# Output projection of a hybrid encoder step: eight turns of a row tile's normalised rows move in between the last matmuls of the next tile

## The reference, cut to what matters

```python
mix = merge_branches(o_fox, o_swa, ga, gb, w_proj_fox[l], w_proj_swa[l], w_o[l])   # ends in ... @ w_o
xp = xp + rmsnorm(mix, norm_mix_post[l])
f, conv_state = conv_ffn(rmsnorm(xp, norm_ffn_pre[l]), zero_past, w_up[l], conv_w[l], conv_b[l], w_down[l])
```

## Time and profile before

| | us |
|---|---|
| median of 3 runs | 1555.41 |
| lowest, highest | 1554.9, 1557.6 |
| span of the profiled execution | 1553.1 |

### The profile page before, as it was taken

One profiled execution on the slowest core, in us unless ns is written; L12 is line 12 of the kernel. 1 busy time (PEld: TensorE's weight loads), 2 busy tenths in 40 slices (PEclk: granted clock), 3 DMA queues, 4 the chain that ended last, 5 costly groups with the idle time before them and its releaser, 6 DMA issues.

```text
span 1553.1 us, 25753 instructions
## 1 busy us (share of the span) xinstructions
PE 1495.8 (96%) x9803; PEld 1397.5 (90%) x9803; DVE 1020.4 (66%) x2016; ACT 607.5 (39%) x1256; POOL 611.0 (39%) x407
## 2 busy tenths in 40 slices
PE   6999999999999999999999999999999999999997
PEld 5889999999997998899788999999999999778885
DVE  6866667767674357867445896555555555578986
ACT  5143534435342235666223333333333332444463
POOL 6522232222222322225231568888888781000104
PEclk9999999999999999999999999999999999999999
DMA  6232222222132721129431122222222228723568
GB/s 199 63 94 74 74 87 65 73 70 70 30 97 75 233 95 38 56 82 291 156 108 58 45 67 86 83 83 83 70 83 68 71 83 278 240 97 116 170 195 156
DMA packets 156475, 165.41 MB, mean 107 GB/s; under 512 B 14005, under 2 KB 121913, under 8 KB 156353
## 3 DMA queue, kind: packets, MB, share of 16 engines
q1 hardware_dynamic: 119689, 109.34, 22.6%
q10 hardware_dynamic: 34840, 51.14, 10.0%
q0 software_dynamic: 1824, 3.28, 1.5%
HBM read 125.56 MB, written 39.85 MB: 107 GB/s over the span
## 4 chain that ended last, share of the span: by engine, by line
PE 80%; DVE 9%; DMA 3%; POOL 3%; ACT 2%; issue 2%; ACTq 1%; SPq 0%; DVEq 0%; POOLq 0%
PE bank L1138 16%; PE bank L1140 16%; PE bank L1139 16%; PE bank L1144 6%; PE bank L1146 6%; PE bank L1145 6%; PE bank L1170 4%; PE bank L1279 2%; PE bank L1250 1%; PE bank L1249 1%; DVE p L2649 1%; DVE rowsn L2408 1%; DVE p L2625 1%; POOL ring_l L1080 1%; PE bank L1629 1%
## 5 line engine op out<-in xcount | busy, mean ns | idle before, releaser
L1138 PE MATMUL bank<-ht_h,ring_h 128*128 128x352 f32 x816 | 268.9, 330 | 1.8 <-POOL ring_l L961 1.1
L1140 PE MATMUL bank<-ht_h,ring_l 128*128 128x352 f32 x816 | 263.2, 323 | 0.0
L1139 PE MATMUL bank<-ht_l,ring_h 128*128 128x352 f32 x816 | 262.6, 322 | 0.0
L960 POOL TENSOR_TENSOR ring_h<-raw,att 128x1024 fp32r<-128x1024 f32 x42 | 86.5, 2059 | 405.6 <-PE bank L1140 396.8
L1138 PE MATMUL bank<-m_h,ring_h 128*128 128x264 f32 x648 | 184.2, 284 | 1.2 <-DVE m_l L2895 1.2
L1139 PE MATMUL bank<-m_l,ring_h 128*128 128x264 f32 x648 | 184.2, 284 | 0.0
L1140 PE MATMUL bank<-m_h,ring_l 128*128 128x264 f32 x648 | 183.9, 284 | 0.0
L1138 PEld LDWEIGHTS bank<-ht_h,ring_h 128*128 128x128 f32 x816 | 153.8, 189 | 5.3 <-issue 2.0
L1139 PEld LDWEIGHTS bank<-ht_l,ring_h 128*128 128x128 f32 x816 | 154.6, 189 | 0.7
L1140 PEld LDWEIGHTS bank<-ht_h,ring_l 128*128 128x128 f32 x816 | 153.9, 189 | 0.0
L1138 PE MATMUL bank<-tb_h,ring_h 128*128 128x264 f32 x456 | 129.9, 285 | 0.2 <-DVE u2s L2909 0.2
(11 more groups left out here) (383 smaller groups left out, 3844.9 us busy)
## 6 DMA issues: line engine op xcount, KB each, us to landing
raw<-in_w_up SPq DMA_DIRECT2D x44, 512.0 KB, 3.9
raw<-in_w_in SPq DMA_DIRECT2D x34, 512.0 KB, 3.9
rb<-in_w_down SPq DMA_DIRECT2D x66, 256.0 KB, 2.9
d_y<-conv SPq DMA_DIRECT2D x22, 529.0 KB, 3.3
d_gate<-gst ACTq DMA_DIRECT2D x48, 176.0 KB, 1.9
a<-d_y SPq DMA_DIRECT2D x33, 256.0 KB, 6.1
ra<-d_y SPq DMA_DIRECT2D x33, 256.0 KB, 3.1
gm<-d_gate ACTq DMA_DIRECT2D x8, 528.0 KB, 4.4
```

The source lines that it names most:

```text
L960: order.link(nc.gpsimd.tensor_tensor(high, src, zero.to_broadcast(list(src.shape)), ALU.add))
L1138: nc.tensor.matmul(out, wh, xh, start=start, stop=False, skip_group_check=onto)
L1139: nc.tensor.matmul(out, wh, xl, start=False, stop=False, skip_group_check=onto)
L1140: return nc.tensor.matmul(out, wl, xh, start=False, stop=stop, skip_group_check=onto)
```

## The change

In tiles 1 to 7 the eight turns of tile t - 1 no longer follow the last matmul of tile t. They are issued one by one behind each of the last nine matmuls of the second half but the final one: a turn behind every matmul of steps k = 5 and 6 and behind the first two of k = 7. The wait for `h_rows` stands before the first turn, the waits for `t_free` before the first and the fifth. The turns of tile 7 (behind the sample tile) and of the sample tile stay where they were. What is computed is the same, with the same number of instructions.

```diff
+            def mix_turn(t, j):
+                if j == 8:
+                    return
+                e, k = divmod(j, 4)
+                if j == 0:
+                    assert ti[0] == T_MIX + 2 * t
+                    pe.wait_ge(h_rows, H_PRE + t + 1)
+                if k == 0:
+                    pe.wait_ge(t_free, T_MIX + 2 * t + e - 1)
+                mm = nc.tensor.transpose(tbank(T_MIX + 2 * t + e)[:, P * k:P * k + P], h2n[:, P * j:P * j + P], ident)
+                if k == 3:
+                    mm.then_inc(t_full, 1)
+                    ti[0] += 1
...
+                        turns = t >= 1 and e == 1 and k >= KT - 3
...
                         else:
-                            mm = three_moving(mix_bank(t, e)[0:r, :], m_h[:, k, P * t:P * t + r],
-                                              m_l[:, k, P * t:P * t + r], wh, wl, k == 0, last)
-                    mm.then_inc(mixed, 1)
-                if t >= 1:
+                            out = mix_bank(t, e)[0:r, :]
+                            th, tl = m_h[:, k, P * t:P * t + r], m_l[:, k, P * t:P * t + r]
+                            nc.tensor.matmul(out, th, wh, start=k == 0, stop=False)
+                            if turns:
+                                mix_turn(t - 1, 3 * (k - KT + 3))
+                            nc.tensor.matmul(out, th, wl, start=False, stop=False)
+                            if turns:
+                                mix_turn(t - 1, 3 * (k - KT + 3) + 1)
+                            mm = nc.tensor.matmul(out, tl, wh, start=False, stop=last)
+                            if last:
+                                mm.then_inc(mixed, 1)
+                            if turns:
+                                mix_turn(t - 1, 3 * (k - KT + 3) + 2)
+                if t == NT:
                     mix_transposes(t - 1)
```

More of the change, by code:

```diff
@@ L1495, in _ @@
                             mm = nc.tensor.matmul(out, both, wl, start=False, stop=last)
-                        else:
-                            mm = three_moving(mix_bank(t, e)[0:r, :], m_h[:, k, P * t:P * t + r],
-                                              m_l[:, k, P * t:P * t + r], wh, wl, k == 0, last)
-                    mm.then_inc(mixed, 1)
-                if t >= 1:
+                            if last:
+                                mm.then_inc(mixed, 1)
+                        else:
+                            out = mix_bank(t, e)[0:r, :]
[7 more added lines that the diff above has]
+                            mm = nc.tensor.matmul(out, tl, wh, start=False, stop=last)
+                            if last:
+                                mm.then_inc(mixed, 1)
+                            if turns:
+                                mix_turn(t - 1, 3 * (k - KT + 3) + 2)
+                if t == NT:
                     mix_transposes(t - 1)
```

## The result

| | before | after |
|---|---|---|
| median of 20 runs each, us | 1555.16 | 1560.38 |
| lowest to highest | 1551.89 to 1560.16 | 1554.2 to 1565.22 |
| ratio, 95% interval | | 1.0028, 1.0017 to 1.0038 |
| span of the profiled execution | 1553.1 | 1557.2 |

The change made the kernel slower by 0.28%, 2.6 to 5.9 us. The forecast was +2.4 us, just under the interval. The medians stand 5.2 us apart, and 1560.38 lies 0.7 us above the upper end of the forecast range, 1559.7. A second set (12 runs of the changed kernel, 35 of the one before) gave 1.0010, 0.9997 to 1.0023. Both sets together are the subject of the first experiment.

The account below looks back on a forecast made before the run. TensorE, busy 96% of the span, was taken to bound the kernel. Terms 0 + 0.2 + 1.3 + 0.9 = +2.4 us, with the median 2.3 us above the span, gave 1557.8 us, range 1554.6 to 1559.7.

Parts of the forecast that it names:

- 1, the single turn: Output projection: 56 moved turns cost 0.109 us each as in a row, term 0; matmuls behind them add 0.2 us.
- two bounds at 0.11 us: For a turn between matmuls: its own streaming, and the load of the product weights behind it, both at 0.11 us.
- the sum: All terms for the moved turns added: 0 + 0.2 + 1.3 + 0.9 = +2.4 us on the span of 1553.1.
- rival (a): Turns between matmuls get cheap, 0.061 us each, their load hidden: -0.3 us in all, 1555.1 us; 10%.
- 2, the stalls: First turns in tiles 2 and 4 wait for slow row writes of tiles 1 and 3: 0.67 us, twice, +1.3 us.
- Rival (b): Late rows of tiles 1 and 3 don't stall, DVE coming ahead of POOL: +1.1 us, 1556.5 us; 8%.
- 3, the lost cover: Turns of tile 6 no longer run beside tile 7's chain, so the wait for `h2n` grows by 0.87 us.
- (c): Alternating turns and product matmuls itself costs; with 0.03 us each, +3.7 us, 1559.1 us; 12%.
- (d): A stall makes the granted clock fall, losing 1.7 us of matmul work: 1559.5 us; 5%.
- the 0.2% line: For the whole kernel, about 0.2% (3.1 us) is what a measurement can tell from no change.
- my cases: Chances for the whole kernel: slower by over 0.2% 0.21, faster by over 0.2% 0.04, within 0.75.
- my own list: Signs of being wrong: unstalled beat under 11.8 or over 12.3 us, 1.28 us row write, shift shrinking before the end.

Follow-up runs that it names:

- the first experiment: The changed kernel run once more, unaltered, against the kernel before: output-projection stage 94.88 us, ratio 1.0010 (0.9997 to 1.0023).
- The kernel with the rounded single turns: Changed kernel with its turns in the products' rounded format, lower-precision part left out: stage 94.66 us.
- the rounded turn ahead of the sample tile: Last turn of a row in the kernel before with normalised rows written and turned in the rounded format: stage 91.20 us.
- The late split: Changed kernel, but POOL splits the weight slabs behind tiles 1 and 3 only once that tile's normalised rows are written: stage 93.61 us, ratio 0.9995.
- the earlier turns: Changed kernel with the single turns one step k earlier, the wait behind 37 matmuls instead of 40: stage 96.18 us.
- the control: Kernel before, with only POOL's weight-slab split delayed until the tile's normalised rows are written: stage 92.37 us.
- the turns in a row: Changed kernel, but a tile's eight turns stand together ahead of the next tile's last matmul: stage 93.25 us, ratio 0.9994.

## Why the prediction was right

**1, the single turn.** The forecast was that a turn costs the same alone as in a row, on the ground of one turn at 183.15 and of two bounds at 0.11 us. It holds for the pair: 0.345 us against 0.341, with 0.004 us more, the value taken from between the ends (by the beats 0.3 us for 56 turns in the changed kernel, where the sum had 0.2). It doesn't hold in the detail to look for, "0.11 us from the turn's start to the next weight load": this reads 0.13, and the matmul behind it 0.22 instead of 0.24. The rule of the Trainium skill, TensorE: Matmul & The Clock Gate (Part 2), that the next weights load while the present matmul runs, was the ground of rival (a). The traces agree with it as far as the turn's own load goes. But it cuts the other way too: behind a turn there is little time to hide the product's load of 0.11 us. The kernel with the rounded single turns shows this. The 55.6 ns that the Trainium skill gives there for a matmul of 128 columns agrees with the 0.06 us of the rounded turn ahead of the sample tile, the one place here with a load of 64 columns behind a rounded turn. Rival (a) is refuted.

**2, the stalls.** Right in place, number and size. 0.67 us in tiles 2 and 4: the beats are longer by 0.66 and 0.65 than their neighbours'. The late split removes both, the earlier turns double them, and the control shows that the slow write alone costs nothing. Rival (b) is refuted. The rule of the Trainium skill, SBUF — State Buffer (Who interferes with whom), that VectorE with two SBUF inputs and a GpSimd instruction that reads SBUF exclude each other, agrees: the write takes 2.91 us beside a split and 1.29 without one. That the exclusion is complete is not shown: the prediction's 3.1 us by it is 0.2 us more than the 2.91 measured.

**3, the lost cover.** Right: 0.87 us forecast; 0.88 with the turns in a row, 0.89 and 1.14 by taking this part back (from 94.86 to 93.97 and from 93.61 to 92.47; the second has 8 single turns fewer, at 0.004 us not enough for the 0.27 us above the forecast, which stay open).

**The sum.** 1.33 + 0.87 + 0.2 = 2.4 against 1.3 + 0.87 + 0.3 = 2.49 us in the trace and 2.3 (standard error 0.3) over the runs with a listed clock once it is taken out. For the stage the mechanism was right, and the size too. The median of 1557.8 us was 2.6 us too low.

**Rivals (c) and (d).** Alternation (c) doesn't cost 0.03 us a turn but 0.002 to 0.007, and neither trace of the changed kernel shows a fall of the clock in the stage (d). The first set's 0.28% is above the 0.2% line all the same, the second set's 0.10% is below it. By my cases, slower by over 0.2% had 0.21, and neither mechanism took place in these traces. What carried the first set there is in part the sampling of the clock, which the forecast didn't reckon with, and in part open (first experiment): I took "about 2.3 us above the span" from one trace and three runs, while single executions of one kernel differ by 8 to 11 us.

**What the profile was to show.** Marks before the first turn in tiles 2 and 4 and nowhere else, 0.8 us more before the turns of tile 7 (1.2 against 0.35 us), beats of 12.0 and 12.7: all seen. The marks were 0.45 us where I had "about 0.5". The shift of the rest can't be read as I meant it: ahead of the stage the changed kernel is 2.4 us late already, since its clock falls at other places. Behind the stage it goes from 4.9 us late to 4.1 at the end. By my own list a shift that shrinks would be wrong. No fall of the clock lies there while TensorE works, in either trace, so the clock isn't the reason. But the stretch from the stage to the end takes 704.7 us in the kernel before, 703.9 and 705.1 in the two traces of the changed kernel, and 703.8 to 705.5 in all fourteen, whichever kernel it is. The 0.7 us are within this scatter, and nothing shows that the change is given back.

## What to carry to other kernels

A turn between long matmuls has two floors, its own stream and the load of the weights of the matmul behind it; taking it out of a row only hides its own load, so look which of the three sets the row before spreading it. When a consumer is moved forward, take the rarest, slowest case of its producer (here 2.91 instead of 1.28 us, in two of the seven tiles whose turns moved): the engine that waits in order pays whatever exceeds the work ahead of the wait, 0.67 us here; and ask of the moved work what it used to cover.

## What was not expected of the hardware

- Loads of weights with 64 rows did not run beside matmuls with 128 rows: the load started 0.32 us after the matmul before it got the array (780.01 to 780.33), and 56 single turns of this kind cost about 16 us of stage, 0.28 us each.
- In the rounded format a turn's weights are recorded with 140 ns, as in float32, and turns in a row come every 0.084 us; a product matmul's weights, in the same format, take 188 ns.
- The time of an execution follows its loss of clock, 0.77 us for each us lost. Each execution has another selection of falls, also in code that is the same, but the places recur: near 17, 471, 499, 611, 639 and 744 us of the span in several of the fourteen traces each.
